# Interleaving the high and low halves of a kernel's input tile, without its spare columns

## The chip, the cores and the metric

The kernel runs on one core of a Trainium2 chip. The metric is the device time of one execution in microseconds (us). Three runs of the kernel before took 3034.17, 3031.98 and 3030.95 us; the median is 3031.98 us.

## The reference

Two layers are computed in float32 on 256 tokens of width 2048, with 16 extra tokens in front of the first layer. The parts that matter here are the large products:

```python
# layer 1: u = rms_norm(h); 2048 -> 4096 product, gate, depthwise convolution, layer norm, silu, 2048 -> 2048 product
u = swiglu(rms_norm(h, norm_ffn_pre), ffn_w_gate, ffn_w_up, ffn_w_down)   # 2048 -> 2 x 5632 -> 2048
def swiglu(h, w_gate, w_up, w_down):
    return (jax.nn.silu(h @ w_gate) * (h @ w_up)) @ w_down
# layer 2: attention with a forget gate, a multiscale pool and two branch gates on one input
proj = h @ w_in                                  # q, k, v, forget, pool input, gates
x = x + merged @ w_out
# then product-key retrieval: q = xn @ w_query, top 16 of 16384 experts in each of 8 heads, and per token
#   a = u_rows . xn ; hid = gelu(a) * gate ; out = sum(hid * v_rows)
```

The answer is the 256 x 2048 result of both layers.

## The kernel before

**Split products.** Most large products run in three passes of a reduced-precision float type (`fp32r` in the profile). Each operand is split into a high part and a low part. ScalarE makes the high part of a weight panel (`split_hi`, L627), VectorE the low part (`split_lo`, L1127), and TensorE adds high x high, high x low and low x high in `product` (L1824 to L1828). A panel is 128 partitions x 2048 floats, 1 MB. SP loads panels in order into four buffers `s_raw` (L463, L464); the split ones lie in two buffers `s_w_hi` and two `s_w_lo`.

**The input tile.** The tile `s_a` (L261) holds the input of a product, 2048 features as KT = 16 k-tiles of 128 partitions. Its layout is `[128, 2, KT, L]`: first all high rows, then all low rows, each k-tile L = 272 columns apart, of which T = 256 are used. `a_hi` and `a_lo` are its two halves. A high row of k-tile k therefore starts 1088 x k bytes into the tile, and its low row lies 17,408 bytes behind it. At L495 GpSimd clears the 16 spare columns of the low half.

**Who reads it.** There are three ways.

- In the gate and up products of the feed-forward layer (`ffn`, L1981, with `double=True`) the function `doubled` (L1830) streams both rows of a k-tile in one matmul of 512 columns against the high weights (L1832), and then the high row alone, 256 columns, against the low weights (L1833). The 512 columns are two runs of 256 in the tile (L1895). There are 1,408 such pairs: 11 rounds of 8 panels of 16. Bank halves are added later by VectorE (L1349). The down product of the same round takes its input from other tiles, `s_h_hi` and `s_h_lo`, whose rows are 1024 bytes apart, as the stationary operand, and streams 512 columns of weights.
- In the products `qk`, `pin`, `gates` and `query` (`feature_major`, L1849) `product` streams 256 columns of a row of the tile three times: high, low, high. There are 1,152 such triples: 256 in `qk`, 128 in `pin`, 512 in the gates, 256 in `query`. The branch products are built in the same way, with the same panels, from the tiles `s_at_hi`, `s_at_lo`, `s_po_hi` and `s_po_lo`, whose rows are 1024 bytes apart.
- In `token_major` (L1872: the products `w_out`, `v` and `w_out_2`) 128 tokens of the tile are the stationary operand and 512 columns of weights are streamed. There are 304 such triples.

**The order around it.** TensorE's instructions are in one fixed order, and each panel waits for its low part. Each round of the feed-forward layer begins while VectorE still adds the eight banks of the round before to `s_yrow` (L1387, L1389) ahead of the next `split_lo`.

**After the last product.** The retrieval stage needs the unsplit input, high plus low, as `s_xnt` (L335), which lies where `a_hi` lies. VectorE adds it in place in two instructions (L1768 to L1771). `xnt_ready` lets TensorE start on the dense experts (L2215) and GpSimd use more buffers (L595). After that VectorE begins with the dot products of the gathered rows (L1703). The gathers are issued by GpSimd (L582, L600), 8 KB a row, and fill five buffers `s_u` and eight `s_v`. Two of the `s_v` lie behind `s_xnt`, at offsets that are written out by hand (L332, L333).

Of the kernel before, what the change touches and what calls it, by code (L numbers as in the profile page):

```python
# [23 lines left out]
T, META = 256, 16  # L24
TT = T // 128
KT = D // 128
L = META + T
# [186 lines left out]
def two_layers(nc, stream, dense_u, columns, x, meta, b_out, g_mix_post, g_ffn, g_ffn_post, g_norm1, g_norm2, w_forget,  # L214
               forget_bias, group_w, keys, expert_u, expert_v, out):
    f32, f32r, u32 = mybir.dt.float32, mybir.dt.float32r, mybir.dt.uint32
    ACT, ALU, AX = mybir.ActivationFunctionType, mybir.AluOpType, mybir.AxisListType


    K, Q = 1024, 32  # L220
# [3 lines left out]
    def place(name, shape, offset, dt=f32):  # L224
        assert name not in names
        names.add(name)
        return nc.alloc_sbuf_tensor_at(name, shape, dt, offset=offset)

    def keep(name, shape, dt=f32):
        nonlocal at  # L230
        t = place(name, shape, at, dt)
        at += (int(np.prod(shape[1:])) * 4 + 63) // 64 * 64
        return t
# [23 lines left out]
    ring0 = at  # L257
    raw = [keep(f"s_raw{i}", [128, 2048]) for i in range(4)]
    w_hi = [keep(f"s_w_hi{i}", [128, 2048], f32r) for i in range(2)]
    w_lo = [keep(f"s_w_lo{i}", [128, 2048], f32r) for i in range(2)]  # L260
    a_both = keep("s_a", [128, 2, KT, L], f32r)  # L261
    a_hi, a_lo = a_both[:, 0], a_both[:, 1]
    S = at
    a_f = place("s_a_f", [128, KT, L], S - 2 * ((KT * L * 4 + 63) // 64 * 64))

    xs = place("s_xs", [128, TT, D], S + 16 * K)
    xs0 = place("s_xs0", [128, TT, D], S + 0)
# [61 lines left out]

    ha = place("s_ha", [128, DENSE, T], S + 24 * K)  # L330
    u_slot = [place(f"s_u{i}", [128, D], before_group if i == 0 else ring0 + (1 + i) * 8 * K) for i in range(NU)]
    free = [S + 8 * K, ring0 - 8 * K, ring0 + 48 * K, ring0 + 56 * K, S + 56 * K, ring0 + 64 * K + (KT * L * 4),  # L332
            ring0 + 72 * K + (KT * L * 4), ring0 - 16 * K]  # L333
    v_slot = [place(f"s_v{i}", [128, D], free[i]) for i in range(NV)]
    xnt = place("s_xnt", [128, KT, L], ring0 + 64 * K)  # L335
    xn_late = place("s_xn_late", [128, D], ring0 + 64 * K)
    xres_late = place("s_xres_late", [128, D], ring0 + 72 * K)
    out_row = place("s_out_row", [128, TT, D], S + 24 * K)
# [42 lines left out]
    with ExitStack() as ctx:  # L381
        bank = [ctx.enter_context(nc.psum_tensor(f"bank{b}", [128, 512], f32)) for b in range(8)]

        def sem(name):
            return ctx.enter_context(nc.semaphore(name))
# [10 lines left out]
        pool_step = sem("pool_step")  # L396
# [31 lines left out]
        xnt_ready, res_taken = sem("xnt_ready"), sem("res_taken")  # L428
# [58 lines left out]
        def _(pool):  # L487
            n = Counts()
# [3 lines left out]
            pool.memset(tri_ones[:, :], 1.0).then_inc(pool_step, 1)  # L492
            pool.memset(causal[:, :], 0.0).then_inc(pool_step, 1)
            pool.iota(inv_count_i[:, :], pattern=[[1, 16]], base=1, channel_multiplier=0).then_inc(pool_step, 1)
            pool.memset(a_lo[:, :, T:L].bitcast(f32), 0.0).then_inc(pool_step, 1)  # L495
            n.base["pool_step"] = 6
            pool.wait_ge(pool_step, n.base["pool_step"])
            pool.affine_select(out=ident[:, :], in_=ident[:, :], compare_op=ALU.not_equal, fill=1.0,
                               base=0, pattern=[[-1, 128]], channel_multiplier=1).then_inc(const_ready, 1)
# [39 lines left out]
            for g, w in enumerate(POOL_WINDOWS):  # L539
                src, s = pin[:, 2 * g:2 * g + 2, :], 1  # L540
                own = src
                for k in range(g + 1):
                    dst = (win_a, win_b)[k % 2][:, :, :]
# [5 lines left out]
                some = mixed[:, 2 * g:2 * g + 2, :]  # L549
# [554 lines left out]
        def _(dve):  # L1104
            n = Counts()
# [501 lines left out]
            for i in range(4):  # L1607
                with n.rounds(dve, "w_out_2"):
# [3 lines left out]
                    for t in range(TT):  # L1612
# [4 lines left out]
                        dst = xres[:, t, i * 512:(i + 1) * 512]  # L1617
# [61 lines left out]
            def gates_softmax(th):  # L1679
                mine = picked[th // PH][:, 2 * SLOTS + th % PH * TOPK:][:, 0:TOPK]  # L1680
                dve.wait_ge(gate_exp, th + 1)
                link(dve.reciprocal(gsum[:, 2:3], gsum[:, 1:2]))
                link(dve.tensor_scalar(mine, gate[:, :], gsum[:, 2:3], None, ALU.mult))
                first_key = picked[th // PH][:, th % PH * TOPK:][:, 0:TOPK]
                dve.scalar_tensor_tensor(gate_kept[th][:, :], first_key, float(SPARSE), mine, ALU.is_lt, ALU.mult).then_inc(gates_ready, 1)
# [79 lines left out]
            best_pairs()  # L1765
            pairs_experts(2)
            dve.wait_ge(panel_used, NPANELS + 1)
            for half in range(2):  # L1768
                some = slice(half * 8, (half + 1) * 8)
                ins = dve.tensor_tensor(xnt[:, some, 0:T], a_hi[:, some, 0:T].bitcast(f32), a_lo[:, some, 0:T].bitcast(f32), ALU.add)  # L1770
            ins.then_inc(xnt_ready, 1)  # L1771
            gates_softmax(2)
            for two in range(4):
                with n.rounds(dve, "keys_6" if two % 2 else "keys_4"):
# [37 lines left out]
        def _(pe):  # L1812
            n = Counts()
# [16 lines left out]
            def doubled(dst, left, both, start, stop):  # L1830

                pe.matmul(dst, left[0], both, start=start, stop=False)  # L1832
                return pe.matmul(dst[:, 0:T], left[1], both[:, 0], start=False, stop=stop)  # L1833

            def marks():

# [12 lines left out]
            def feature_major(banks, tokens, c0, panels, kper, k, only=None, ready=None, between=None, double=False):  # L1849

                width = len(banks) * 128
                for c in only or range(panels):
                    s = panel(c0 + c)
                    for j, b in enumerate(banks):
                        for kk in range(kper):
                            kt = c * kper + kk
                            if kt == 0:
                                into(b, k)
                            if between and (c, j, kk) in between:
                                between[c, j, kk]()  # L1860
                            if ready and j == 0 and kt % 4 == 0:
                                pe.wait_ge(bank_empty[4 + kt // 4], ready[kt // 4])
                            where = slice(kk * width + j * 128, kk * width + (j + 1) * 128)
                            right = tokens(kt)
                            left, ends = (w_hi[s][:, where], w_lo[s][:, where]), (kt == 0, kt == panels * kper - 1)
                            ins = doubled(bank[b][:, :], left, right, *ends) if double else product(bank[b][:, 0:T], left, right, *ends)
                        if j == len(banks) - 1:
                            ins.then_inc(panel_used, 1)
                        elif c == panels - 1:
                            ins.then_inc(bank_full[b], 1)  # L1870
# [21 lines left out]
                return a_hi[:, k, 0:T], a_lo[:, k, 0:T]  # L1892

            def both_tokens(k):
                return a_both[:, :, k, 0:T]  # L1895

            pe.wait_ge(const_ready, 3)
            with n.rounds(pe, "norm0"):
                pe.wait_ge(meta_scaled, 1)
                for k in range(KT):  # L1900
                    ins = pe.transpose(bank[7][:, k * META:(k + 1) * META], meta_sb[:, k * 128:(k + 1) * 128], ident[0:META, 0:META])
                ins.then_inc(panel_used, 1)
                for t, ready in ((0, xs_ready), (1, xs_late_ready)):
                    for b in range(4):
# [3 lines left out]
                        for q in range(4):  # L1908
                            k = 4 * b + q
                            ins = pe.transpose(bank[4 * t + b][:, q * 128:(q + 1) * 128], xs0[:, t, k * 128:(k + 1) * 128], ident[:, :])  # L1910
# [19 lines left out]
            for k in range(2):  # L1930
                ins = pe.matmul(bank[2][:, 0:T], ones[:, :], cvo[:, k, :], start=k == 0, stop=k == 1)
# [49 lines left out]
            def ffn(between, ready):  # L1981

                for blk in range(2):
                    feature_major((4 * blk, 4 * blk + 1), both_tokens, 4 * blk, 2, 8, 0, ready=None if blk else ready,
                                  between=None if blk else between, double=True)
                    feature_major((4 * blk + 2, 4 * blk + 3), both_tokens, 4 * blk + 2, 2, 8, 0, double=True)
                for f in range(4):
                    s = panel(8 + f)
                    pe.wait_ge(hlo_ready, n.after("hlo", f + 1))
                    for t in (1, 0):  # L1990
                        for c in range(4):
                            b = c if t else 4 + c
                            if f == 0:
                                into(b, 1)
                            tile, where = slice(t * 128, (t + 1) * 128), slice(c * 512, (c + 1) * 512)
                            ins = product(bank[b][:, :], (h_hi[:, f, tile], h_lo[:, f, tile]),
                                          (w_hi[s][:, where], w_lo[s][:, where]), f == 0, f == 3)
                            if f == 3 and b < 7:
                                ins.then_inc(bank_full[b], 1)
                    ins.then_inc(panel_used, 1)  # L2000
# [39 lines left out]
            with n.rounds(pe, "forget"):  # L2040
                pe.wait_ge(wf_loaded, 16)
                into(6, 0)
                for k in range(0, KT, 4):
                    for term, a in enumerate((a_hi, a_lo)):
                        for q in range(4):
                            ins = pe.matmul(bank[6][q * Q:(q + 1) * Q, 0:T], wf_raw[:, k + q, :], a[:, k + q, 0:T].bitcast(f32),
                                            start=k == 0 and term == 0, stop=k == KT - 4 and term == 1)
# [332 lines left out]
```

## Time and profile before

| | |
|---|---|
| median of three runs | 3031.98 us |
| the profiled execution, its own time | 3026.89 us |
| its span, first to last instruction | 3024.8 us |
| TensorE busy | 2633.5 us (87%) |
| VectorE busy | 1887.5 us (62%) |
| ScalarE busy | 1177.2 us (39%) |
| GpSimd busy | 853.5 us (28%) |
| mean granted TensorE clock | 0.934 |

The profiled execution took 2.1 us more than its span. An engine's share says how long it was busy over the whole span. It doesn't say which engine set the end of a stage; for that the busy time of one stretch, and what ended the idle time in it, are read. Matmuls are pipelined: the listed length of one (394 ns) is longer than the distance from its start to the next start, and only that distance counts for the time. Starts are printed to 10 ns, so a distance is read over many matmuls.

### The profile page before, as it was taken

To read this page: it belongs to the slowest core of one execution; us is meant where nothing else is said; L and a number is where in the kernel's file an instruction comes from. 1 tells how busy PE (TensorE), PEld (TensorE's weight loads), DVE (VectorE), ACT (ScalarE), POOL (GpSimd) and SP (SyncE) were. 2 spreads that over 40 slices of the span, in tenths; PEclk is the share of its full clock that TensorE was granted. 3 is DMA by queue.
4 is the path that set the end of the run, shared out by engine and by line. 5 is a ranking of instruction groups with operands and counts; after the bars stand their busy time and mean duration, and the time that the engine had idled before them with its cause. 6 is when DMAs were issued, how large, how long until landed. Compare 5 with 4: busy or idle time off the path is not lost.

```text
span 3024.8 us, 40065 instructions
## 1 busy us (share of the span) xinstructions
PE 2633.5 (87%) x14748; PEld 2022.0 (67%) x14748; DVE 1887.5 (62%) x2592; ACT 1177.2 (39%) x2290; POOL 853.5 (28%) x568
## 2 busy tenths in 40 slices
PE   8999899999999989999999999888865566777673
PEld 7886788888888878989999898666542322222220
DVE  6888566565565664464445468888677764454455
ACT  1003443334343343435334444655455532222233
POOL 0000000000000000040000003555568887776675
PEclk9999999999999999999999999999876688988987
DMA  6343545555555543443545657999999999999998
GB/s 242 139 144 107 208 155 193 181 193 182 192 186 189 190 170 137 158 146 144 186 180 201 230 206 273 407 417 409 398 354 391 391 390 405 421 410 423 419 415 348
DMA packets 128586, 796.59 MB, mean 263 GB/s; under 512 B 30546, under 2 KB 30546, under 8 KB 31762
## 3 DMA queue, kind: packets, MB, share of 16 engines
q0 software_dynamic: 75712, 417.94, 34.3%
q1 hardware_dynamic: 52736, 376.90, 33.9%
q8 instruction: 75, 1.23, 0.2%
q14 instruction: 63, 0.52, 0.1%
HBM read 923.45 MB, written 4.19 MB: 307 GB/s over the span
## 4 chain that ended last, share of the span: by engine, by line
PE 53%; DMA 16%; DVE 13%; issue 9%; POOL 7%; ACT 2%; DVEq 1%; POOLq 0%; SPq 0%; ACTq 0%
DMA s_u<-in_expert_u,s_u_index 10%; PE bank L1832 10%; PE bank L1826 10%; PE bank L1827 10%; PE bank L1828 9%; DMA s_v<-in_expert_v,s_v_index 5%; PE bank L1833 5%; PE bank L1922 4%; DVE s_u L1703 4%; POOL s_v L600 3%; POOL s_u L582 3%; PE bank L2275 2%; DVE s_cacc L1216 2%; DVE s_w_lo L1127 1%; DVE s_yrow L1389 1%
## 5 line engine op out<-in xcount | busy, mean ns | idle before, releaser
L1127 DVE TENSOR_TENSOR s_w_lo<-s_raw,s_w_hi 128x2048 fp32r<-128x2048 f32 x258 | 592.5, 2297 | 577.8 <-ACT s_w_hi L627 577.4
L627 ACT ACTIVATE s_w_hi<-s_raw 128x2048 fp32r<-128x2048 f32 x256 | 490.4, 1916 | 750.8 <-PE bank L1828 475.3
L2275 PE MATMUL bank<-s_v,s_spread 128*32 128x512 f32 x2048 | 318.1, 777 | 313.0 <-DMA s_v<-in_expert_v,s_v_index 308.1
L1832 PE MATMUL bank<-s_a,s_w_hi 128*128 128x512 f32 x1408 | 494.4, 394 | 3.2 <-DVE s_w_lo L1127 3.2
L600 POOL DMA_INDIRECT s_v<-in_expert_v,s_v_index x256 | 414.9, 1621 | 187.1 <-PE bank L2275 83.0
L582 POOL DMA_INDIRECT s_u<-in_expert_u,s_u_index x256 | 388.4, 1517 | 263.6 <-DVE s_adot L1703 120.7
L1703 DVE CUSTOM_DVE_ANT_0 s_u<-s_u,s_xn_late 128x2048 f32<-128x2048 f32 x128 | 293.6, 2294 | 270.0 <-DMA s_u<-in_expert_u,s_u_index 269.8
L2275 PEld LDWEIGHTS bank<-s_v,s_spread 128*32 128x32 f32 x2048 | 83.3, 138 | 523.1 <-issue 516.9
L1049 ACT ACTIVATE s_spread<-s_ident,s_hid 32x32 f32<-32x32 f32 x1024 | 325.6, 318 | 231.4 <-DVE s_hid L1742 219.0
L1833 PE MATMUL bank<-s_a,s_w_lo 128*128 128x256 f32 x1408 | 395.2, 281 | 0.0
L1703 DVE CUSTOM_DVE_ANT_0 s_u<-s_u,s_xn 128x2048 f32<-128x2048 f32 x128 | 292.8, 2290 | 82.4 <-DMA s_u<-in_expert_u,s_u_index 81.1
L1826 PE MATMUL bank<-s_a,s_w_hi 128*128 128x256 f32 x1152 | 325.4, 282 | 3.4 <-DVE s_a L1151 1.8
L1827 PE MATMUL bank<-s_a,s_w_hi 128*128 128x256 f32 x1152 | 324.7, 282 | 0.0
L1828 PE MATMUL bank<-s_a,s_w_lo 128*128 128x256 f32 x1152 | 324.2, 281 | 0.0
L1832 PEld LDWEIGHTS bank<-s_a,s_w_hi 128*128 128x128 f32 x1408 | 264.7, 188 | 66.3 <-DVE s_w_lo L1127 6.4
L1833 PEld LDWEIGHTS bank<-s_a,s_w_lo 128*128 128x128 f32 x1408 | 265.3, 188 | 0.4
L1922 PE MATMUL bank<-s_a_f,s_raw 128*128 128x272 f32 x1024 | 235.2, 393 | 3.2 <-DVE s_a_f L1184 2.4
L2232 PE MATMUL bank<-s_raw,s_ha 128*128 128x512 f32 x512 | 226.7, 598 | 0.0
L1922 PEld LDWEIGHTS bank<-s_a_f,s_raw 128*128 128x128 f32 x1024 | 194.6, 190 | 43.5 <-issue 3.8
L1826 PEld LDWEIGHTS bank<-s_a,s_w_hi 128*128 128x128 f32 x1152 | 218.0, 189 | 7.9 <-issue 3.8
L527 POOL MEMSET s_row_of<- 16x2048 f32 x1 | 1.8, 1798 | 773.4 <-DVE s_xs L1300 773.4
L1828 PEld LDWEIGHTS bank<-s_a,s_w_lo 128*128 128x128 f32 x1152 | 218.5, 190 | 0.0
(320 smaller groups left out, 3800.5 us busy)
## 6 DMA issues: line engine op xcount, KB each, us to landing
s_raw<-in_stream SPq DMA_DIRECT2D x292, 1024.0 KB, 4.8
s_raw<-in_expert_v SPq DMA_DIRECT2D x32, 1024.0 KB, 8.9
s_raw<-in_dense_u SPq DMA_DIRECT2D x29, 1024.0 KB, 8.9
s_u<-in_expert_u,s_u_index POOLq DMA_INDIRECT x256, 14.5
s_v<-in_expert_v,s_v_index POOLq DMA_INDIRECT x256, 14.8
s_panel_early<-in_dense_u POOLq DMA_DIRECT2D x3, 1024.0 KB, 11.4
s_xres<-in_x SPq DMA_DIRECT2D x2, 1024.0 KB, 5.9
out<-s_out_row SPq DMA_DIRECT2D x8, 256.0 KB, 4.6
```

The source lines that it names most:

```text
L582: pool.indirect_dma_start(u_slot[k % NU][:, :], None, expert_u, index, bounds_check=SPARSE * NKEYS - 1, oob_is_err=False).then_inc(u_loade ...
L600: pool.indirect_dma_start(v_slot[k % NV][:, :], None, expert_v, index, bounds_check=SPARSE * NKEYS - 1, oob_is_err=False).then_inc(v_loade ...
L627: act.activation(w_hi[s % 2][:, :], raw[s][:, :], ACT.Copy).then_inc(hi_ready, 1)
L1127: dve.tensor_tensor(w_lo[s % 2][:, :], raw[s][:, :], w_hi[s % 2][:, :].bitcast(f32), ALU.subtract)\
L1703: dve.tensor_tensor_reduce(out=u_slot[k % NU][:, :], in0=u_slot[k % NU][:, :], in1=xn_late[:, :] if t else xn[:, 0, :], scale=SHRINK, scal ...
L1826: pe.matmul(dst, left[0], right[0], start=start, stop=False)
L1827: pe.matmul(dst, left[0], right[1], start=False, stop=False)
L1828: return pe.matmul(dst, left[1], right[0], start=False, stop=stop)
L1832: pe.matmul(dst, left[0], both, start=start, stop=False)
L1833: return pe.matmul(dst[:, 0:T], left[1], both[:, 0], start=False, stop=stop)
L1922: ins = pe.matmul(bank[c][:, 0:L], raw[c % 4][:, k * 128:(k + 1) * 128], a_f[:, k, :], start=k == 0, stop=k == KT - 1)
L2275: ins = pe.matmul(bank[4 * t + c][q * Q:(q + 1) * Q, :], spread[g % NW][:, q, :], v_slot[(4 * g + q) % NV][:, c * 512:(c + 1) * 512], star ...
```

## The change

The tile becomes `[128, KT, 2, T]`: high row and low row of a k-tile lie next to each other, and the 16 spare columns are gone. Rows are 256 floats, so high rows start 2048 x k bytes into the tile and low rows 1024 bytes behind them. The 512 columns of the wide matmul are one run. Every tile behind it, all those placed from `S`, moves down by 2 KB. `s_xnt` no longer lies on its own source element by element, so the sum is made in five instructions of 1, 1, 2, 4 and 8 k-tiles, each behind the one before (`link` signals a semaphore and waits for it). The clearing of the spare columns is removed, and the offsets of two gather buffers follow the smaller tile.

```diff
-    a_both = keep("s_a", [128, 2, KT, L], f32r)
-    a_hi, a_lo = a_both[:, 0], a_both[:, 1]
+    a_both = keep("s_a", [128, KT, 2, T], f32r)
+    a_hi, a_lo = a_both[:, :, 0], a_both[:, :, 1]
     S = at
-    a_f = place("s_a_f", [128, KT, L], S - 2 * ((KT * L * 4 + 63) // 64 * 64))
+    a_f = place("s_a_f", [128, KT, L], S - 2 * KT * T * 4)
...
-    free = [S + 8 * K, ring0 - 8 * K, ring0 + 48 * K, ring0 + 56 * K, S + 56 * K, ring0 + 64 * K + (KT * L * 4),
-            ring0 + 72 * K + (KT * L * 4), ring0 - 16 * K]
+    free = [S + 8 * K, ring0 - 8 * K, ring0 + 48 * K, ring0 + 56 * K, S + 56 * K, ring0 + 64 * K + (KT * T * 4),
+            ring0 + 72 * K + (KT * T * 4), ring0 - 16 * K]
...
-    xnt = place("s_xnt", [128, KT, L], ring0 + 64 * K)
+    xnt = place("s_xnt", [128, KT, T], ring0 + 64 * K)
...
-            pool.memset(a_lo[:, :, T:L].bitcast(f32), 0.0).then_inc(pool_step, 1)
-            n.base["pool_step"] = 6
+            n.base["pool_step"] = 5
...
-            for half in range(2):
-                some = slice(half * 8, (half + 1) * 8)
-                ins = dve.tensor_tensor(xnt[:, some, 0:T], a_hi[:, some, 0:T].bitcast(f32), a_lo[:, some, 0:T].bitcast(f32), ALU.add)
-            ins.then_inc(xnt_ready, 1)
+            for k0, k1 in ((0, 1), (1, 2), (2, 4), (4, 8), (8, 16)):
+                some = slice(k0, k1)
+                added = dve.tensor_tensor(xnt[:, some, :], a_hi[:, some, :].bitcast(f32), a_lo[:, some, :].bitcast(f32), ALU.add)
+                if k1 < KT:
+                    link(added)
+            added.then_inc(xnt_ready, 1)
...
-                return pe.matmul(dst[:, 0:T], left[1], both[:, 0], start=False, stop=stop)
+                return pe.matmul(dst[:, 0:T], left[1], both[:, 0, :], start=False, stop=stop)
...
-                return a_both[:, :, k, 0:T]
+                return a_both[:, k]
```

## Rows read from the trace of the kernel before

**Rows 1.** Busy time by stretch: start:end, length, PE busy (instructions), granted clock, DMA share, GB/s.

```profile
382.00:1100.00 718.00, 714.81 (x3794) 1.00 0.52 186
1650.00:1739.00 89.00, 89.00 (x387) 1.00 0.63 236
1880.00:3020.00 1140.00, 809.20 (x3975) 0.84 0.98 400
```

**Rows 2.** Waits, longest first, 1860 to 3024 us: total, times, longest.

```profile
DVE s_u L1703 <- DMA s_u<-in_expert_u,s_u_index: 350.9, 173, 5.6
PE bank L2275 <- DMA s_v<-in_expert_v,s_v_index: 308.1, 51, 14.2
```

**Rows 3.** TensorE in order of time, second feed-forward round: start us, length us, engine, line.

```profile
457.59 0.49 PE L1832 MATMUL bank<-s_a,s_w_hi 128*128 128x512 f32 x1 [0.37 <-DVE s_w_lo L1127]
...
496.79 0.40 PE L1826 MATMUL bank<-s_w_hi,s_h_hi 128*128 128x512 f32 x1
```

**Rows 4.** TensorE in order of time, two neighbouring pairs, k-tiles 4 and 5.

```profile
598.76 0.40 PE L1832 MATMUL bank<-s_a,s_w_hi 128*128 128x512 f32 x1
...
599.12 0.39 PE L1832 MATMUL bank<-s_a,s_w_hi 128*128 128x512 f32 x1
...
599.46 0.40 PE L1832 MATMUL bank<-s_a,s_w_hi 128*128 128x512 f32 x1
```

**Rows 5.** TensorE in order of time, a down product: first and last of 96 matmuls.

```profile
563.83 0.40 PE L1826 MATMUL bank<-s_w_hi,s_h_hi 128*128 128x512 f32 x1
...
585.40 0.39 PE L1828 MATMUL bank<-s_w_hi,s_h_lo 128*128 128x512 f32 x1
```

**Rows 6.** TensorE in order of time, a branch product's 96 matmuls and the first behind them.

```profile
1501.62 0.28 PE L1826 MATMUL bank<-s_po_hi,s_w_hi 128*128 128x256 f32 x1
...
1513.13 0.28 PE L1826 MATMUL bank<-s_a,s_w_hi 128*128 128x256 f32 x1
```

**Rows 7.** TensorE in order of time, gates: 384 matmuls and the first behind them.

```profile
1444.66 0.28 PE L1826 MATMUL bank<-s_a,s_w_hi 128*128 128x256 f32 x1
...
1490.11 0.28 PE L1826 MATMUL bank<-s_at_hi,s_w_hi 128*128 128x256 f32 x1
```

**Rows 8.** TensorE in order of time, three qk panels: first and last of 192 matmuls.

```profile
1175.99 0.39 PE L1826 MATMUL bank<-s_a,s_w_hi 128*128 128x256 f32 x1
...
1198.70 0.28 PE L1828 MATMUL bank<-s_a,s_w_lo 128*128 128x256 f32 x1
```

**Rows 9.** TensorE in order of time, w_out_2: first and last of 384 matmuls.

```profile
1650.09 0.40 PE L1826 MATMUL bank<-s_w_hi,s_a 128*128 128x512 f32 x1
...
1738.83 0.39 PE L1828 MATMUL bank<-s_w_hi,s_a 128*128 128x512 f32 x1
```

**Rows 10.** Groups by line and form, VectorE: count, busy us, mean ns, idle before.

```profile
L1357 DVE TENSOR_TENSOR s_hf<-s_hf,s_sg 128x256 f32<-128x256 f32 x44 | 16.6, 419 | 0.0
...
L1669 DVE TENSOR_TENSOR s_pick<-s_iota_f,s_pos_of 128x512 f32<-128x512 f32 x16 | 11.1, 692 | 0.5
...
L1528 DVE TENSOR_TENSOR s_a<-s_merged,s_a 128x1024 fp32r<-128x1024 f32 x4 | 4.8, 1219 | 0.0
...
L1770 DVE TENSOR_TENSOR s_xnt<-s_a 128x2048 f32<-128x2048 f32 x2 | 4.5, 2284 | 0.0
```

**Rows 11.** In order of time, VectorE and TensorE from 1844 to 1873 us.

```profile
1844.17 0.69 DVE L1669 TENSOR_TENSOR s_pick<-s_iota_f,s_pos_of 128x512 f32<-128x512 f32 x1
...
1844.90 0.69 DVE L1671 TENSOR_TENSOR s_pick<-s_pick,s_ind 128x512 f32<-128x512 f32 x1
...
1846.64 4.49 DVE L1770 TENSOR_TENSOR s_xnt<-s_a 128x2048 f32<-128x2048 f32 x2
...
1852.35 20.88 PE L2223 MATMUL bank<-s_xnt,s_panel_early 128*128 128x256 f32 x96
```

**Rows 12.** In order of time, the start: the clearing, and VectorE's first real work.

```profile
1.68 0.30 POOL L495 MEMSET s_a<- 128x256 f32 x1
...
5.95 0.15 DVE L1166 RECIPROCAL s_stat<-s_stat 16x1 f32<-16x1 f32 x1 [2.43 <-ACT s_stat L670]
```

**Rows 13.** Groups by tile `s_a`, ScalarE and VectorE: count, shortest/median/longest ns, first and last start.

```profile
L660 ACT ACTIVATE s_a<-bank x24: 592/597/600, 380.1 to 1751.1; 128x512 fp32r<-128x512 f32 x24
L1151 DVE TENSOR_TENSOR s_a<-bank,s_a x24: 678/682/691, 380.8 to 1753.2; 128x512 fp32r<-128x512 f32 x24
```

## The prediction, made before the changed kernel was run

> **What bounds the kernel now.** I read the busy time by stretch first. From 382 to 1100 us, the feed-forward layer, TensorE is busy for 714.81 of 718 us, in the last split product for 89.00 of 89, at full granted clock in both [rows 1]. After 1880 us it is busy for 809 of 1140 us, DMA stands at a share of 0.98, and the waits there are for gathered rows [rows 1, 2]. So up to about 1845 us the distance between the starts of two matmuls sets the time; behind that the gathers do. The gathers start when the products are done, so what the first part gains or loses reaches the end whole, and nothing that is gained on TensorE behind 1850 us counts.
>
> The change touches no count of matmuls or columns. It moves addresses, so the question is whether the distance between starts depends on them. I read this from the timeline, over stretches without a wait.
>
> - Wide pairs (512 + 256 columns): 112 pairs from 457.59 to 496.79 us, 39.20/112 = 350.0 ns a pair [rows 3].
> - 512 columns with all rows on multiples of 512 bytes (down product): 21.57 us/95 = 227.1 ns [rows 5].
> - 512 columns of weights against the tile `s_a`, whose rows are 1088 bytes apart: 88.74/383 = 231.7 ns [rows 9].
> - 256 columns of tiles with rows 1024 bytes apart: 11.51/96 = 119.9 ns [rows 6].
> - 256 columns of `s_a`: 45.45/384 = 118.4 ns in the gates [rows 7], 22.71/191 = 118.9 ns in qk [rows 8].
>
> So addresses do matter, by 1 to 5 ns a matmul, and in both directions. On even addresses 512 columns take 4.6 ns less and 256 columns 1 to 1.6 ns more. These two even values fit one form: columns at 2.4 GHz, the granted level, plus 13.4 to 13.8 ns (512/2.4 = 213.3, 256/2.4 = 106.7).
>
> Within the wide pairs there is a pattern. From the starts of all L1832 after the first panel of each round I worked out the mean pair by k-tile modulo 4, that is by the row's start modulo 256 bytes (1088 = 4 x 256 + 64): 352.0, 345.4, 348.1 and 351.3 ns. Two pairs of one panel show it as 0.36 and 0.34 us [rows 4]. All four have the break between their two runs, and the class at 345.4 lies below 227.1 + 119.9 = 347.0. The break itself thus costs nothing that I can see; what costs is where a run starts.
>
> **The change part by part.** All sums are against the profiled execution, 3026.89 us (span 3024.8 and 2.1 around it), 5.1 us below the median of the three runs.
>
> *The wide pairs.* One run of 512 on even addresses and one of 256 on even addresses: I take 227.1 + 119.9 = 347.0, 3.0 ns less, over 1,408 pairs -4.2 us. The first panel of each round doesn't gain: TensorE is held up by VectorE's low part right behind it, 0.37 us in the round shown [rows 3], because the bank sums go first; 10 rounds x 16 pairs x 3.0 ns = 0.5 us is given back as a longer wait. Term: -3.7 us. Bounds: below, 227.1 plus half of it for 256 columns, 340.6 ns, -9.4 x 1,408 = -13.2, less 1.5 given back, -11.7 us. Above, the class whose rows start even already, 352.0 ns: +2.0 x 1,408 = +2.8 us. I take the value between, since it is made of two stretches that run steadily on even addresses, whereas in the class at 352.0 the neighbours are uneven.
>
> The Trainium skill ("TensorE: Matmul & The Clock Gate", section "Back-to-back issue gap") gives a distance of N/2.4 + 2.5 ns for N columns at full clock, with no word on where the operand lies. That would be 325 ns for the pair; the trace has 350, so it disagrees on the size. By its form layout is free, which is the third rival below. "SBUF — State Buffer" (section "Specifications (TRN2)") of the Trainium skill adds that each step to a new 16-byte line costs. One run in place of two saves a single such step in 512 columns, which speaks against the change; no row here shows a cost of one step.
>
> *The triples of 256 columns.* The tile's rows become even, as those of the branch products are, with the same panels and the same function. Gates: 512 x 3 x (119.9 - 118.4) = +2.3 us. qk, pin and query: 640 x 3 x (119.9 - 118.9) = +1.9 us. Term: +4.2 us. Bounds: 0 if the distance doesn't move, and down to -17 us if it fell to 113.5, half of 227.1; the branch products show steady 119.9 with even rows, so I take that and keep little of the lower end.
>
> *The token-major triples.* Stationary rows become even, as in the down product, which streams the same weight buffers: 912 matmuls x (231.7 - 227.1) = -4.2 us. Bounds: 0 and -4.2, since 227.1 is the lowest of any stretch of 512.
>
> *The sum for `s_xnt`.* Five linked instructions of 256, 256, 512, 1024 and 2048 elements: 419 + 419 + 692 + 1219 + 2284 ns = 5.03 us by the group rows [rows 10]; a linked one starts 0.04 us behind the end of the one before (1844.17 + 0.69 to 1844.90, [rows 11]), so four links add 0.16. Sum 5.19 us against 4.49 us for the two that overlap [rows 11]: +0.7 us. What is queued behind: VectorE's gate sums and its first dot products, for whose buffers GpSimd's gathers wait. TensorE doesn't wait: the sum is ready at 1851.1 us and it reaches the first dense panel at 1852.35 [rows 11], so 0.7 fits. I take +0.7 us on the path; bounds 0 (the gathers hide it) and +0.7.
>
> *The rest.* The clearing on GpSimd (0.30 us) goes, but VectorE then waits until 5.95 us for ScalarE anyway [rows 12]: 0. If that cover were gone it would be -0.3. Writes into the tile by ScalarE (597 ns) and VectorE (682 ns) keep their sizes and get another step between rows [rows 13]; they spread 592 to 600 and 678 to 691 ns over all steps used, so 0, bounds +-0.2 us for the few that TensorE waits on. Moving 2 KB down changes no start modulo 1024 of the other tiles: 0. The dense experts' matmuls lie in the part paced by DMA: 0, and the bytes gathered are the same.
>
> Sum: -3.7 + 4.2 - 4.2 + 0.7 = -3.0 us. Profiled execution 3023.9 us, median **3029.0 us**.
>
> **The rivals.**
>
> *A, the wide run streams freely (faster).* The 256 columns behind an even run of 512 take 113.5 and not 119.9 ns: -11.7 + 4.2 - 4.2 + 0.7 = -11.0 us, 3021.0 us. For it: the down product holds 227.1 without a tremor, and one class of pairs is at 345.4 already. Against: no stretch of 256 columns in the trace is below 118.4.
>
> *B, even rows are the bad case (slower).* When moving row and weights start on the same offset modulo 256 bytes, both reads meet. The place is every matmul on `s_a`; the pairs go to the 352.0 of their even class (+2.8), the triples to 119.9 (+4.2), the token-major ones don't gain (0), the sum costs 0.7: +7.7 us, 3039.7 us. It decides from the point where pairs lie above 350. For it: the k-tiles that are even today are the dearest, and the branch products too are dearer than the gates. Against: the down product, even throughout, is the cheapest.
>
> *C, the layout does nothing.* The distances stay, since they come from what VectorE, ScalarE and DMA do beside them: only +0.7, 3032.7 us. Against: four classes of k-tile inside one panel differ by up to 6.6 ns under the same load.
>
> **How the numbers follow.** Forecast 0.42, A 0.19, B 0.20, C 0.19. About 6 us, 0.2%, is what a measurement of this kernel can tell from no change. The forecast has its own range of -9 to +2, since the pair and the triples each may be 2 ns off; a quarter of it lies beyond -6. Faster by over 0.2%: 0.10 + 0.18 of A = 0.28. Slower: 0.14 of B and 0.02 elsewhere = 0.16. Within: 0.56. Range: from 3018 (a little below A) to 3041 (a little above B); the forecast's own is 3023 to 3034.
>
> **What would show it.** In the new timeline, pairs at 347 ns with no pattern over k-tiles (A: 341, B: 352, C: the same four classes); the triples on `s_a` at 120.0 instead of 118.4; w_out_2 at 227 instead of 231.7, its 384 matmuls 1.8 us shorter. Five L1770 successors summing to 5.2 us. The stage behind 1850 us as long as before, 1178 us. I am wrong if pairs or triples leave 345 to 350 or 118 to 120.5 ns, or if the gathering part changes its length by more than 3 us, which none of these terms does.

## The result, and the profile after

The changed kernel is slower, by 0.2%. Twelve runs of each on one chip gave a median of 3036.07 us (3032.32 to 3045.02) against 3030.72 us (3026.79 to 3034.84) for the kernel before. The ratio is 1.0021, 95% interval 1.0011 to 1.0031. The forecast was 3029.0 us, 3.0 us below the median then shown, in a range of 3018 to 3041. The time lies in the range, but it moved the other way.

The profiled execution took 3034.25 us, its span is 3032.2 us. Busy time by stretch, to be held against [rows 1], shows full clock and a busy TensorE as before, with 19 matmuls fewer in the same 718 us of the feed-forward layer (the stretch from 1650 now begins in the branch product, so its count can't be compared):

```profile
382.00:1100.00 718.00, 715.56 (x3775) 1.00 0.52 185
1650.00:1739.00 89.00, 89.00 (x417) 1.00 0.63 237
1880.00:3020.00 1140.00, 812.20 (x3965) 0.84 0.99 401
```

TensorE in order of time, in the stretches that answer to [rows 3, 5, 7, 8, 9], each first and last (line numbers are one higher). Columns: start us, length us, engine, line. The last row is the last matmul of the last product.

```profile
455.13 0.50 PE L1833 MATMUL bank<-s_a,s_w_hi 128*128 128x512 f32 x1 [0.30 <-DVE s_w_lo L1126]
...
494.80 0.40 PE L1827 MATMUL bank<-s_w_hi,s_h_hi 128*128 128x512 f32 x1
...
562.30 0.40 PE L1827 MATMUL bank<-s_w_hi,s_h_hi 128*128 128x512 f32 x1
...
583.86 0.39 PE L1829 MATMUL bank<-s_w_hi,s_h_lo 128*128 128x512 f32 x1
...
1178.48 0.39 PE L1827 MATMUL bank<-s_a,s_w_hi 128*128 128x256 f32 x1
...
1201.51 0.28 PE L1829 MATMUL bank<-s_a,s_w_lo 128*128 128x256 f32 x1
...
1448.17 0.28 PE L1827 MATMUL bank<-s_a,s_w_hi 128*128 128x256 f32 x1
...
1494.25 0.28 PE L1827 MATMUL bank<-s_at_hi,s_w_hi 128*128 128x256 f32 x1
...
1655.53 0.40 PE L1827 MATMUL bank<-s_w_hi,s_a 128*128 128x512 f32 x1
...
1742.37 0.39 PE L1829 MATMUL bank<-s_w_hi,s_a 128*128 128x512 f32 x1
...
1849.99 0.28 PE L1829 MATMUL bank<-s_a,s_w_lo 128*128 128x256 f32 x1
```

| step between starts | before | forecast | after |
|---|---|---|---|
| wide pair, 112 in the second round | 350.0 ns | 347.0 | 39.67/112 = 354.2 |
| down product (not touched) | 227.1 | 227.1 | 21.56/95 = 226.9 |
| triples in the gates, a matmul | 118.4 | 119.9 | 46.08/384 = 120.0 |
| triples in qk, a matmul | 118.9 | 119.9 | 23.03/191 = 120.6 |
| w_out_2, a matmul | 231.7 | 227.1 | 86.84/383 = 226.7 |

The last product's last matmul starts at 1849.99 us; before it was 1845.26, so 4.7 us later. Along the way the marks are these: 1.8 us earlier at the first pair (behind w_out), 2.2 us later behind the feed-forward layer, 5.4 us later at w_out_2, 3.5 behind it, 4.7 at the end. The remaining 2.7 us of the 7.4 us between the two profiled spans lie behind the last product.

In the first feed-forward round the pairs ran otherwise than in the ten later ones. TensorE in order of time, five successive wide matmuls of that round, 0.34 to 0.35 us apart:

```profile
408.85 0.39 PE L1833 MATMUL bank<-s_a,s_w_hi 128*128 128x512 f32 x1
409.20 0.39 PE L1833 MATMUL bank<-s_a,s_w_hi 128*128 128x512 f32 x1
409.55 0.39 PE L1833 MATMUL bank<-s_a,s_w_hi 128*128 128x512 f32 x1
409.89 0.39 PE L1833 MATMUL bank<-s_a,s_w_hi 128*128 128x512 f32 x1
410.24 0.39 PE L1833 MATMUL bank<-s_a,s_w_hi 128*128 128x512 f32 x1
```

Over whole panels of 16, from the third panel of a round on, the step is 346.7 ns there and 353.3 ns in every later round (15 steps from the first to the last pair of a panel: 5.20 and 5.30 us; the first panel of a later round has 352.7, the second holds the wait for its low part). The pattern over k-tiles is gone in both.

VectorE's sum of the two halves, the answer to the 4.49 us in [rows 11]:

```profile
1851.24 5.18 DVE L1769 TENSOR_TENSOR s_xnt<-s_a 128x256 f32<-128x256 f32 x5
```

### The profile page after: what moved, and what is told of

It is laid out like the page before. It is cut to its first block, busy times and chain, and to the rows that moved or that the text cites. A ratio compares the mean times of both kernels' runs of the same rounds, so it can differ in the third digit from the quotient of the medians.

```text
span 3032.2 us, 40067 instructions
## 1 busy us (share of the span) xinstructions
PE 2644.3 (87%) x14748; PEld 2029.6 (67%) x14748; DVE 1888.6 (62%) x2595; ACT 1177.3 (39%) x2290; POOL 857.6 (28%) x567
## 4 chain that ended last, share of the span: by engine, by line
PE 52%; DMA 14%; DVE 13%; issue 10%; POOL 8%; ACT 2%; DVEq 1%; POOLq 0%; SPq 0%; ACTq 0%
PE bank L1833 10%; PE bank L1827 10%; DMA s_u<-in_expert_u,s_u_index 10%; PE bank L1829 9%; PE bank L1828 9%; PE bank L1834 5%; DMA s_v<-in_expert_v,s_v_index 4%; POOL s_u L581 4%; POOL s_v L599 4%; PE bank L1923 4%; DVE s_u L1702 4%; DVE s_cacc L1215 2%; PE bank L2276 2%; DVE s_w_lo L1126 1%; DVE s_yrow L1388 1%
## 5 line engine op out<-in xcount | busy, mean ns | idle before, releaser
L581 POOL DMA_INDIRECT s_u<-in_expert_u,s_u_index x256 | 401.2, 1567 | 265.9 <-DVE s_adot L1702 117.8
L599 POOL DMA_INDIRECT s_v<-in_expert_v,s_v_index x256 | 406.5, 1588 | 184.7 <-PE bank L2276 80.9
L1833 PEld LDWEIGHTS bank<-s_a,s_w_hi 128*128 128x128 f32 x1408 | 264.6, 188 | 70.4 <-DVE s_w_lo L1126 5.6
L1834 PEld LDWEIGHTS bank<-s_a,s_w_lo 128*128 128x128 f32 x1408 | 266.1, 189 | 0.4
L1827 PEld LDWEIGHTS bank<-s_a,s_w_hi 128*128 128x128 f32 x1152 | 221.6, 192 | 7.7 <-issue 3.9
L2233 PE MATMUL bank<-s_raw,s_ha 128*128 128x512 f32 x512 | 226.7, 597 | 0.0
L1828 PEld LDWEIGHTS bank<-s_a,s_w_hi 128*128 128x128 f32 x1152 | 221.7, 192 | 0.1
```

Source lines behind the costliest of these rows:

```text
L581: pool.indirect_dma_start(u_slot[k % NU][:, :], None, expert_u, index, bounds_check=SPARSE * NKEYS - 1, oob_is_err=False).then_inc(u_loade ...
L599: pool.indirect_dma_start(v_slot[k % NV][:, :], None, expert_v, index, bounds_check=SPARSE * NKEYS - 1, oob_is_err=False).then_inc(v_loade ...
L1827: pe.matmul(dst, left[0], right[0], start=start, stop=False)
L1828: pe.matmul(dst, left[0], right[1], start=False, stop=False)
L1834: return pe.matmul(dst[:, 0:T], left[1], both[:, 0, :], start=False, stop=stop)
```

## The experiments

**Even rows without the joined run.** The rows are 1024 bytes apart, but high and low halves stay apart, as in the kernel before.

```diff
-    a_both = keep("s_a", [128, KT, 2, T], f32r)
+    a_both = keep("s_a", [128, 2, KT, T], f32r)     # two runs; sum in two instructions
```

> The rows of the input tile start on even addresses (1024 bytes apart, no spare columns), but all high rows lie ahead of all low rows, so the wide matmul still streams two runs of 256; the sum for the retrieval stage is the old one of two instructions. Theory (even starts): the wide pairs behave as in the changed kernel, 354 ns a pair in rounds 2 to 11 and 347 in the first; narrow triples at 120 to 120.5 ns a matmul, w_out_2 at 227. Only the longer sum is gone, so about 0.7 us below the changed kernel: ratio to the kernel before about 1.0018. Rival (the joined run costs): the wide pairs go back to about 350 or below, -5.9 us against the changed kernel, ratio about 1.000.

Measured: ratio 1.0013 (1.0004 to 1.0022). The timeline of this kernel has 39.67/112 = 354.2 ns a pair in the second round:

```profile
454.73 0.50 PE L1831 MATMUL bank<-s_a,s_w_hi 128*128 128x512 f32 x1 [0.30 <-DVE s_w_lo L1126]
...
494.40 0.40 PE L1825 MATMUL bank<-s_w_hi,s_h_hi 128*128 128x512 f32 x1
```

The triples take 120.0 ns in the gates and 120.4 to 120.7 in qk, w_out_2 226.7, and the last product's last matmul starts at 1849.61 us. All that the change did to TensorE is there without the joined run.

**The joined run without even rows.** The 16 spare columns go behind each pair of rows. (Left out below: the tiles behind it are placed anew to make room.)

```diff
-    a_both = keep("s_a", [128, KT, 2, T], f32r)
+    a_both = keep("s_a", [128, KT, 2 * T + 16], f32r)
```

> High and low row of a k-tile lie next to each other, one run of 512, but with 16 spare columns behind each pair (2112 bytes from pair to pair), so that starts go through four classes modulo 256 bytes as in the kernel before. Theory (even starts): pairs at 349 to 350 ns with a pattern over k-tiles modulo 4, triples at 118.4 to 118.9, w_out_2 at 231.7: the kernel before plus the 0.7 us of the longer sum, ratio about 1.000. Rival (the joined run costs): pairs at 354, +5.9 us, ratio about 1.002.

Measured: ratio 0.9997 (0.9988 to 1.0007). The timeline of this kernel, round four and one gates stretch: 39.21/112 = 350.1 ns a pair, 45.45/384 = 118.4 ns a matmul.

```profile
592.47 0.50 PE L1835 MATMUL bank<-s_a,s_w_hi 128*128 128x512 f32 x1 [0.32 <-DVE s_w_lo L1128]
...
631.68 0.40 PE L1829 MATMUL bank<-s_w_hi,s_h_hi 128*128 128x512 f32 x1
...
1445.44 0.28 PE L1829 MATMUL bank<-s_a,s_w_hi 128*128 128x256 f32 x1
...
1490.89 0.28 PE L1829 MATMUL bank<-s_at_hi,s_w_hi 128*128 128x256 f32 x1
```

By k-tile modulo 4 the pairs take 352.9, 345.0, 349.2 and 350.0 ns (steps inside the third to eighth panels of all rounds; in the kernel before, read in the same way, 352.4, 345.2, 348.8 and 350.2). With the run before it this parts the two edits: one run of 512 or two of 256 makes no difference, where the rows start does.

**TensorE's later rounds written out.** This asks why the first round ran at 346.7 ns.

```diff
-            with n.rounds(pe, "ffn", FF // 512 - 1):
-                ffn(None, None)
+            for _ in range(FF // 512 - 1):
+                with n.rounds(pe, "ffn"):
+                    ffn(None, None)
```

> The changed kernel with TensorE's ten later feed-forward rounds written out instead of looped; the first round, always written out, ran its pairs at 346.7 ns and the looped ones at 353.3. Theory (the step of the pairs is a locked state set by how a round begins, after a 512-column stretch or after a wait): 353.3 ns stays in the later rounds, time unchanged. Rival (the instruction stream of a loop costs): 346.7 ns in all rounds, 1,280 x 6.6 ns = -8.4 us against the changed kernel, less about 1 us of longer waits: ratio to the kernel before about 0.9995.

Measured: ratio 1.0017 (1.0008 to 1.0027). The timeline of this kernel, second round, has 39.67/112 = 354.2 ns again, so the loop isn't what makes the later rounds slow. The first panel of that round, first and last wide matmul below, still ran at 5.20/15 = 346.7 ns (352.7 in the looped kernel). The slower step set in behind the wait for the low part of the second panel, the third row, and from round three on the first panels had 352.7 too.

```profile
449.62 0.39 PE L1833 MATMUL bank<-s_a,s_w_hi 128*128 128x512 f32 x1
...
454.82 0.39 PE L1833 MATMUL bank<-s_a,s_w_hi 128*128 128x512 f32 x1
...
455.71 0.50 PE L1833 MATMUL bank<-s_a,s_w_hi 128*128 128x512 f32 x1 [0.38 <-DVE s_w_lo L1126]
...
495.38 0.40 PE L1827 MATMUL bank<-s_w_hi,s_h_hi 128*128 128x512 f32 x1
```

**The longer sum alone,** in the kernel before.

```diff
-            for half in range(2):
-                some = slice(half * 8, (half + 1) * 8)
+            for k0, k1 in ((0, 1), (1, 2), (2, 4), (4, 8), (8, 16)):   # each linked to the one before
```

> The kernel before with only its retrieval-input sum made in five linked instructions. Theory: +0.7 us (5.19 against 4.49 us on VectorE), all else as before, the stage behind the last product 0.7 us longer, ratio 1.0002. Rival (it shifts the gathers and costs more behind it): that stage 2.7 us longer, as in the changed kernel, ratio 1.0009.

Measured: ratio 1.0007 (0.9998 to 1.0017), so neither 0.7 nor 2.7 us is told from the other by time. In the profiled execution the part behind the last product is 3026.4 - 1844.93 = 1181.5 us. This part differs between profiled kernels by more than the term: 1179.5 before, 1182.2 after, 1182.2 with even rows apart, 1186.1 with joined uneven rows, and 1178.1 to 1188.0 over all kernels of this study. What the sum costs beyond its own 0.7 us stays open.

**Even rows, moved by 64, 128 and 192 bytes,** in the changed kernel. (Left out below: the tiles behind it are placed anew, clear of it.)

```diff
+    SH = 64     # 128, 192
+    at += SH
     a_both = keep("s_a", [128, KT, 2, T], f32r)
```

> The changed kernel with the whole input tile moved up by 64 bytes: rows still 1024 bytes apart, but all start 64 bytes past a multiple of 256, while weight panels stay on multiples. Theory R (what counts is the offset of the streamed rows against the weights): the pairs take the value of that class in the kernel before, 345.4 ns. Theory S (what counts is that nothing changes from matmul to matmul, so a fixed step sets in, of which there are two): 353.3 again in the later rounds, 346.7 in the first; triples 120.0, w_out_2 226.7.

> The same, moved up by 128 bytes. Theory R: 348.1 ns a pair. Theory S: 353.3 in the later rounds, 346.7 in the first; triples 120.0, w_out_2 226.7.

> The same, moved up by 192 bytes. Theory R: 351.3 ns a pair. Theory S: 353.3 in the later rounds, 346.7 in the first; triples 120.0, w_out_2 226.7.

| rows start at | wide pair, later rounds | triples in gates | triples in qk | w_out_2 | ratio |
|---|---|---|---|---|---|
| 0 (the changed kernel) | 353.3 | 120.0 | 120.6 | 226.7 | 1.0021 |
| +64 | 348.9 or 353.3, by round | 117.8 | 118.3, one stretch 114.1 | 233.3 | 1.0004 (0.9993 to 1.0014) |
| +128 | 351.1 | 118.7 | 119.2 | 232.4 | 1.0015 (1.0005 to 1.0025) |
| +192 | 353.3 | 113.4 | 114.0 | 228.9 (w_out 233.4) | 0.9966 (0.9956 to 0.9977) |

The steps of the pairs are those of the third to eighth panels. Both theories fall. R gave 345.4, 348.1 and 351.3 for the pairs, and none came. S gave unchanged triples and w_out_2, and both moved with the offset. What S had right is that a steady stretch has a fixed step, and that there can be two. The triples show two as well: a panel that ran free had 117.8 or 113.3 ns a matmul, at +64 mostly the first and in the last qk stretch (from 1227.55 us) the second, at +192 mostly the second and in two of the four stretches in query the first. The timeline of the kernel at +64, rounds two and three, shows both with the same instructions on the same addresses, 39.18/112 = 349.8 and 39.68/112 = 354.3 ns. In rounds 2 to 11 of this kernel the first panel had 349.1 ns each time; the step was 348.9 or 353.3 from the third panel to the last of the round, never changing between. The wait between doesn't tell which: it was 0.29 us in rounds of either kind.

```profile
457.80 0.50 PE L1836 MATMUL bank<-s_a,s_w_hi 128*128 128x512 f32 x1 [0.35 <-DVE s_w_lo L1129]
...
496.98 0.40 PE L1830 MATMUL bank<-s_w_hi,s_h_hi 128*128 128x512 f32 x1
...
524.79 0.50 PE L1836 MATMUL bank<-s_a,s_w_hi 128*128 128x512 f32 x1 [0.29 <-DVE s_w_lo L1129]
...
564.47 0.39 PE L1830 MATMUL bank<-s_w_hi,s_h_hi 128*128 128x512 f32 x1
```

And at +192, a gates stretch of 384 matmuls in 43.54 us, 113.4 ns each:

```profile
1445.82 0.29 PE L1830 MATMUL bank<-s_a,s_w_hi 128*128 128x256 f32 x1
...
1489.36 0.28 PE L1830 MATMUL bank<-s_at_hi,s_w_hi 128*128 128x256 f32 x1
```

**Even rows only where the tile is stationary,** that is in w_out and w_out_2, in the kernel before.

```diff
+    a_even = place("s_a_even", [128, 2, KT, T], ring0 + 64 * K, f32r)
...
-            def token_major(banks, only=range(4), ready=None):
+            def token_major(banks, only=range(4), ready=None, hi=e_hi, lo=e_lo):
```

> The kernel before, but in the products w_out and w_out_2, where the tile is only the stationary operand, it is written and read with rows 1024 bytes apart; in all other products the rows stay 1088 bytes apart. Theory: 240 triples x 3 x (231.7 - 226.7) = -3.6 us, the last product ends at 1841.7 instead of 1845.3 us, pairs and narrow triples as before; ratio 0.9988. Rival (writing the tile with another step costs ScalarE or VectorE something that TensorE waits for): the stretch is no shorter, ratio 1.000.

Measured: ratio 0.9988 (0.9977 to 0.9999), last matmul at 1841.76 us, as expected. w_out_2 in this kernel, 86.84/383 = 226.7 ns:

```profile
1648.50 0.40 PE L1828 MATMUL bank<-s_w_hi,s_a_even 128*128 128x512 f32 x1
...
1735.34 0.39 PE L1830 MATMUL bank<-s_w_hi,s_a_even 128*128 128x512 f32 x1
```

**A layout for each product.** The feed-forward input keeps the old rows, w_out and w_out_2 get even ones, and the products with triples, v, and the tiles `s_at_hi` and `s_at_lo` get rows at +192.

```diff
+    mix = place("s_mix", [128, 2, KT, T], ring0 + 64 * K + 192, f32r)
+    even = place("s_even", [128, 2, KT, T], ring0 + 64 * K, f32r)
...
-    at_hi = place("s_at_hi", [128, HEADS, T], S + 61 * K, f32r)
+    at_hi = place("s_at_hi", [128, HEADS, T], S + 61 * K + 192, f32r)
```

> Each product gets the rows that its order of matmuls runs best on in the runs so far. Feed-forward input: the layout of the kernel before (350.0 ns a pair). w_out and w_out_2: even rows (226.7). The products that stream 256 columns three times, and v: rows 1024 bytes apart that start 192 bytes past a multiple of 256 (113.4 to 114 in the kernel moved up by 192), the attention branch's two tiles too; the sum for the retrieval input is the short one. Theory (the step depends on the offset between streamed rows and weights alone): 512 triples x 3 x 5.0 + 640 x 3 x 4.9 + 128 x 3 x 6.5 + 240 x 3 x 5.0 ns = 7.7 + 9.4 + 2.5 + 3.6, less 0.3 in v, = -22.9 us; the last product ends near 1822.5 instead of 1845.3, ratio 0.9925. Rival (the 113.4 came with the place of other tiles in that kernel): the triples stay at 118.4, ratio 0.9988.

Measured: median 3010.47 us, ratio 0.9932 (0.9918 to 0.9945). The last product's last matmul starts at 1827.06 us, 18.2 us earlier and not 22.9. The tiles behind the input tile stayed where they were in the kernel before, but for `s_at_hi` and `s_at_lo`, so the rival, that 113.4 came with their place, falls. The gates stretch of this kernel took 43.54 us for 384 matmuls, 113.4 ns each:

```profile
1437.36 0.29 PE L1839 MATMUL bank<-s_mix,s_w_hi 128*128 128x256 f32 x1
...
1480.90 0.28 PE L1839 MATMUL bank<-s_at_hi,s_w_hi 128*128 128x256 f32 x1
```

The attention branch's stretches ran at 113.3 too (119.9 before). Of the 4.7 us missing, 2.6 us are three stretches in qk and query, 597 matmuls, that held 118.2 to 118.4 ns where their neighbours on the same rows held 114.0. Another 3.1 us are missing in the first gates stretch (1356.1 to 1414.9 us): its 384 matmuls and what runs between them took 58.75 us, against 57.53 before, where 1.9 us less were reckoned. TensorE waits once in it for VectorE's low part, 1.92 us (1.65 before), and right behind that wait the granted clock was 0.50 for 3.4 us, the lower of the two levels:

```profile
1372.74 0.39 PE L1839 MATMUL bank<-s_mix,s_w_hi 128*128 128x256 f32 x1 [1.92 <-DVE s_w_lo L1140]
1373.10:1376.50 3.40, 3.40 (x19) 0.50 0.59 248
```

The second row is a stretch as in [rows 1]. The panel in it took 152.8 ns a matmul. In two of the kernels of the next experiment the same wait was followed by a granted clock of 1.00, that panel took 116.0 ns a matmul, and the whole gates stretch 57.0 us. So the clock cost 1.7 us here. The last three panels of the stretch held 117.8 ns instead of 113.3. What gives back about 1 us elsewhere wasn't traced.

**Different offsets for high and low rows of the pairs,** in that kernel.

```diff
+    ffn_a = place("s_ffn_a", [128, 2, 2064], ring0 + 64 * K + 192, f32r)   # k-tiles 0 to 7: high 192, low 0
+    ffn_b = place("s_ffn_b", [128, 2, 2096], ring0 + 81 * K + 0, f32r)     # k-tiles 8 to 15: high 0, low 192
```

> The same kernel, but the feed-forward input in two halves: for k-tiles 0 to 7 the high rows start 192 bytes past a multiple of 256 and the low rows on one, for 8 to 15 the other way round. Theory (only the high row meets the weight loads, since a load takes less than 256 columns): panels with high rows at 192 run pairs at 340 to 347 ns, those with high rows at 0 at 347 to 353. Rival (the state is set by how a stretch begins): 346.7 or 353.3 in both, whatever the rows.

> The same with high rows at 0 and low rows at 64 for k-tiles 0 to 7, and high at 64, low at 0 for 8 to 15. Theory (the high row decides): 347 to 353 and about 350 ns a pair. Rival (the step from the low row to the next high row decides as well): the two kinds of panel swap or both differ from 350.4 to 354.8, which rows all at 64 gave.

> The same with high rows at 0 and low rows at 128 for k-tiles 0 to 7, and high at 192, low at 64 for 8 to 15. Theory (the high row decides): 347 to 353 and the same value as the panels with high 192 and low 0. Rival: anything else, above all a value of 340, the floor of 226.7 + 113.3.

| k-tiles 0 to 7 / 8 to 15 (high, low) | panels with k-tiles 0 to 7 | with 8 to 15 | ratio, two runs each |
|---|---|---|---|
| 192, 0 / 0, 192 | 346.9 | 346.5 | 0.9920 (0.9901 to 0.9940) |
| 0, 64 / 64, 0 | 346.5 or 350.5 | 346.9 or 347.3 | 0.9927 (0.9905 to 0.9948) |
| 0, 128 / 192, 64 | 349.7 | 347.1 | 0.9924 (0.9905 to 0.9942) |

The steps are those of the third to eighth panels in the later rounds, over 15 pairs of a panel. In the first kernel of the three, round three, those six panels have 33.30/96 = 346.9 ns a pair:

```profile
529.18 0.39 PE L1851 MATMUL bank<-s_ffn_a,s_w_hi 128*128 128x512 f32 x1
...
562.48 0.40 PE L1845 MATMUL bank<-s_w_hi,s_h_hi 128*128 128x512 f32 x1
```

Each value lies in or next to the band that the theory gave, but the theory itself, that the high row alone decides, falls when they are put beside the runs with equal offsets: high at 192 gives 346.9 or 347.1 with low at 0 or 64 and 353.3 with low at 192, and high at 0 gives 346.5, 349.7 and 353.3 with low at 192, 128 and 0. (The reason given with it, that a weight load takes less than 256 columns, no trace shows: the loads are listed with 188 ns.) High and low rows count together. Equal offsets, which the change has, are the dearest choice tried for high rows at 0 and at 192. The rival, a state that doesn't depend on the rows, falls too. The value of 340 didn't come.

By its pairs the first kernel of the three is the fastest, 66.75 us a round against 66.85 to 66.96 and 66.92 in the others, and 67.04 in the kernel before. Its last matmul is still the latest of the three (1824.81 us, then 1824.20 and 1823.51), because it began its pairs 1.1 and 2.4 us later than the others and it alone has the half clock of 3.4 us in the first gates stretch. The times of the three, two runs each, can't be told from one another.

## Why the prediction was wrong

**What bounds the kernel: right.** The feed-forward and mixer stages followed TensorE's steps to a few tenths of a microsecond: from the first pair to the last product's last matmul the pairs' stage gave +3.9 us and the rest +2.6. The gathering part stayed within the spread seen over all runs (1178.1 to 1188.0 us; 1182.2 in the changed kernel).

**The triples, +4.2 us: right in sign, a little small.** 512 x 3 x 1.6 + 640 x 3 x 1.7 ns = 5.7 us. The branch products were the right row for the gates (120.0 for 119.9); qk and query came out at 120.4 to 120.7. Its lower bound, 113.5, was given little weight; the runs at +192 reached 113.4, so that value exists, but not on even rows. (The bound's sum is -17.9 us, not -17.)

**The token-major triples, -4.2 us: right.** 912 x 5.0 = -4.6 us.

**The sum, +0.7 us: right** for the instructions (5.18 us for 5.19).

**The wide pairs, -3.7 us: this step failed.** It said "One run of 512 on even addresses and one of 256 on even addresses: I take 227.1 + 119.9 = 347.0". The first round did run at 346.7, but the ten later ones at 353.3. Over a whole round of 67 us that is 67.50 us against 67.04, +0.46 us, ten times +4.6 us; the first round gave back a little. With the forecast's 347.0 the round would have been shorter. The whole stage came out 3.9 us longer and not 3.7 shorter, beyond the term's upper bound of +2.8, and 353.3 lies outside the 345 to 350 ns that the prediction had set as its own test. The failure is of the method: two steps, each measured in a stretch of its own kind, were added. The runs showed that a mixed stretch has its own step, which differs by 6.6 ns between rounds with the same addresses. The row that came nearest was discounted: the class of k-tiles whose rows were even already took 352.0 ns (352.4 with the trace's unrounded starts), and the even kernel took 353.3. Why a mixed stretch has this step stays open.

**Rival B came about,** in the pairs and triples, though not in the form given: it had the token-major ones gain nothing. With the measured terms, +3.9 for the pairs' stage, +5.7, -4.6 and +0.7, the sum is 5.7 us, and the ratio gives 6.4 (3.3 to 9.4). The time fell into the stated range because the range had been drawn wide enough for this rival. Its reason, that equal offsets are always the bad case, is refuted: w_out_2 is fastest on them.

**Rival C falls:** the steps changed when the rows were moved.

**That the break between two runs is free** was said and is shown, by both halves of the change run alone.

**Two readings beside the sum.** The Trainium skill, "TensorE: Matmul & The Clock Gate", section "Back-to-back issue gap", gives N/2.4 + 2.5 ns for a single isolated matmul, a condition that the prediction didn't say when it set 325 ns beside the 350 of a stream. The Trainium skill, "SBUF — State Buffer", section "Specifications (TRN2)", says that each step to a new 16-byte line costs. One run in place of two saves no such step, where the prediction counted one: by that line size 512 floats fill 128 lines either way. The unchanged step (354.2 ns with one run and with two) is no test of what such a step costs.

## What to carry to other kernels

When an edit moves operands of back-to-back matmuls, read the distance between starts for every pattern of matmuls, and class it by the operand's address modulo 256 bytes; a row of the same pattern at the new address weighs more than a sum of rows of other patterns. Try a few offsets by experiment, for each product by itself: here one layout for all products moved the time by between +0.2% and -0.3% with its offset, and one for each by -0.7% to -0.8%, with no instruction added to any product. Joining two runs of 256 columns into one of 512 gained nothing.

## What the runs showed of the hardware

- The step between matmuls of this type depends on where the rows of the input tile start modulo 256 bytes, with the weights on multiples of 256: 113.4, 117.8, 118.7 or 120.0 ns for 256 columns in the gates, 226.7 to 233.3 for 512, at full granted clock in all of them. The weights were never moved, so whether the offset against them counts, or the address itself, is open.
- The lowest and the highest steady values lie 6.6 or 6.7 ns apart: 113.4 and 120.0; 226.7 and 233.3; 346.7 and 353.3. That is 16 columns, or 64 bytes of floats, at 2.4 GHz; and 113.4 and 226.7 are 17/16 of the time of 256 and 512 columns. Other steady values lie between (117.8 and 118.7; 228.9, 231.7 and 232.4; 348.9 and 351.1). What happens inside in those 16 columns no run shows.
- The same instructions on the same addresses can settle on two steps (348.9 or 353.3 ns at +64; 346.7 and 353.3 at 0; 113.3 or 117.8 for triples at +64 and at +192). In the kernels with one offset for all rows of the tile, the step didn't change between the third panel and the last of a feed-forward round; where it changed, a wait or another kind of matmul lay between. What picks one is open: written-out rounds have the slow one too, and no run varied the way in which a stretch is entered.
- All five kernels whose gates ran on rows at +192 waited 1.92 us for VectorE in the first gates stretch. In three of them 3.4 us at a granted clock of 0.50 followed, which cost 1.7 us; in two the clock stayed at 1.00, as it did in the kernel before, where the wait was 1.65 us.
- No layout tried brought the pairs to 340 ns, the sum of the lowest steps of 512 and 256 columns.
